# Twelve of 32 experts with 64 token slots and two weight products, the gated unit as one ScalarE function, and down weights in 8 KB pieces

## The reference

```python
logits = (hf @ w_router + b_router).astype(jnp.float32)
top_vals, top_idx = lax.top_k(logits, TOP_EXPERTS)     # 4 of 32
gates = jax.nn.softmax(top_vals, axis=-1)
...
gu = xb @ w_gu[e] + b_gu[e]                            # 1024 -> 2048
glu = jnp.minimum(gu[:, :D_EXPERT], SWIGLU_LIMIT)
lin = jnp.clip(gu[:, D_EXPERT:], -SWIGLU_LIMIT, SWIGLU_LIMIT)
act = glu * jax.nn.sigmoid(SWIGLU_ALPHA * glu) * (lin + 1.0)
return (act @ w_down[e] + b_down[e]) * g[:, None]      # 1024 -> 1024
```

## Time and profile before

| what | value |
|---|---|
| median of 3 runs | 1509.83 us |
| span of the profiled execution | 1508.6 us |
| the runs' times less that span | 0.8 to 3.4 us |
| TensorE busy | 1454.6 us, 96% |
| VectorE busy | 1310.3 us, 87% |
| ScalarE busy | 1105.7 us, 73% |
| GpSimd busy | 232.7 us, 15% |
| moved | 448.53 MB |
| granted TensorE clock | full in nearly all of the 40 slices |

### The profile page before, as it was taken

One profiled execution on the slowest core, in us unless ns is written; L12 is line 12 of the kernel. 1 busy time (PEld: TensorE's weight loads), 2 busy tenths in 40 slices (PEclk: granted clock), 3 DMA queues, 4 the chain that ended last, 5 costly groups with the idle time before them and its releaser, 6 DMA issues.

```text
span 1508.6 us, 18823 instructions
## 1 busy us (share of the span) xinstructions
PE 1454.6 (96%) x7148; PEld 1197.1 (79%) x7148; DVE 1310.3 (87%) x1320; ACT 1105.7 (73%) x1197; POOL 232.7 (15%) x120
## 2 busy tenths in 40 slices
PE   6999888999999999999999999999999999999996
PEld 5887767776788888888888888888888888888885
DVE  5799777558899999989999999999999999899995
ACT  5676654456778778887877788787787878887773
POOL 1122000011111121111111121111111211111101
PEclk9999979999999999999999999999999999999999
DMA  5422011178999999999999999999999999999991
GB/s 147 152 58 69 29 56 42 49 280 322 328 370 372 369 368 366 374 368 373 366 370 370 370 372 370 376 364 357 369 368 368 368 364 373 369 368 362 381 359 36
DMA packets 102307, 448.53 MB, mean 297 GB/s; under 512 B 18496, under 2 KB 23616, under 8 KB 69376
## 3 DMA queue, kind: packets, MB, share of 16 engines
q1 hardware_dynamic: 89808, 428.32, 73.4%
q0 software_dynamic: 9792, 18.90, 5.2%
q10 hardware_dynamic: 2608, 0.01, 0.1%
HBM read 440.89 MB, written 23.07 MB: 308 GB/s over the span
## 4 chain that ended last, share of the span: by engine, by line
PE 86%; DVE 9%; ACT 2%; issue 2%; DMA 1%; POOL 0%; POOLq 0%; ACTq 0%; DVEq 0%
PE ps L1948 68%; PE ps L1710 2%; PE ps L1712 2%; PE ps L1711 2%; PE ps L1958 2%; PE ps L1917 2%; PE ps L1722 2%; PE ps L1909 2%; DVE work L1388 1%; DVE nmax L1399 1%; PE ps L1813 1%; DVE top L1387 1%; DVE W L571 1%; DMA out_dram<-ysb 1%; PE ps L1784 0%
## 5 line engine op out<-in xcount | busy, mean ns | idle before, releaser
L776 DVE TENSOR_TENSOR whl<-wraw,whl 128x2048 fp32r<-128x2048 f32 x384 | 865.7, 2288 | 83.4 <-ACT whl L771 74.7
L771 ACT ACTIVATE whl<-wraw 128x2048 fp32r<-128x2048 f32 x384 | 732.8, 1919 | 206.5 <-PE ps L1948 206.5
L1948 PE MATMUL ps<-whl,xT 128*128 128x512 f32 x3120 | 730.6, 392 | 1.3 <-issue 1.3
L1948 PEld LDWEIGHTS ps<-whl,xT 128*128 128x128 f32 x3120 | 580.6, 188 | 122.8 <-issue 2.0
L1948 PE MATMUL ps<-whl,aT 128*128 128x512 f32 x1488 | 346.1, 391 | 0.6 <-DVE whl L776 0.6
L1948 PEld LDWEIGHTS ps<-whl,aT 128*128 128x128 f32 x1488 | 276.9, 188 | 57.0 <-DVE whl L776 1.0
L941 POOL DMA_INDIRECT out_dram<-ysb,idx x32 | 100.6, 3144 | 453.3 <-ACT ysb L1222 453.3
L932 POOL DMA_INDIRECT xg<-h_rows,idx x32 | 88.3, 2759 | 471.2 <-DVE idx L1606 463.6
L1710 PE MATMUL ps<-W,HT 128*128 128x512 f32 (+1 forms) x184 | 73.1, 397 | 5.8 <-DVE W L571 4.8
L1712 PE MATMUL ps<-W,HT 128*128 128x512 f32 (+1 forms) x184 | 70.1, 381 | 0.0
L1711 PE MATMUL ps<-W,HT 128*128 128x512 f32 (+1 forms) x184 | 69.8, 379 | 0.0
(11 more groups left out here) (246 smaller groups left out, 1377.0 us busy)
## 6 DMA issues: line engine op xcount, KB each, us to landing
wraw<-in_w_gu_dram SPq DMA_DIRECT2D x256, 1024.0 KB, 8.1
wraw<-in_w_down_dram SPq DMA_DIRECT2D x128, 1024.0 KB, 7.1
WR<-in_w_in_dram SPq DMA_DIRECT2D x20, 512.0 KB, 3.6
WR<-in_w_o_dram SPq DMA_DIRECT2D x8, 512.0 KB, 3.7
xs<-in_x_dram SPq DMA_DIRECT2D x4, 512.0 KB, 7.9
WR<-in_x_dram SPq DMA_DIRECT2D x4, 512.0 KB, 3.6
out_dram<-WR SPq DMA_DIRECT2D x4, 512.0 KB, 2.6
h_rows<-WR SPq DMA_DIRECT2D x4, 512.0 KB, 2.6
```

The source lines that it names most:

```text
L771: act.activation(whl[:, n % HL, 0, :], wraw[n % RAW], ACT.Copy).then_inc(chunk_hi, 1)
L776: eng.tensor_tensor(whl[:, n % HL, 1, :], wraw[n % RAW], whl[:, n % HL, 0, :].bitcast(F32), ALU.subtract).then_inc(chunk_lo, 1)
L1948: ins = pe.matmul(bank, a[x_][j], w[:, b, j, 512 * q:512 * q + 512], start=c == NG and j == 0 and n == 0, stop=last and j == nj - 1 and n ...
```

## The change

Twelve places in the order of experts (3, 5, 8, 10, 13, 15, 18, 20, 23, 25, 28, 30) become narrow: 64 slots. The experts are sorted by their token count when the program runs, and the twelve with fewest tokens go to the narrow places; experts 0 and 1 stay where they are (`FIXED`). SP reads the expert's number into a register for its loads.

A narrow expert's stationary operand holds the tokens' high parts in columns 0 to 63 and their low parts in columns 64 to 127. Products with the high and the low weights then give rows 0 to 63 and rows 64 to 127, eight matmuls in a chunk. Rows 64 to 127 are added to rows 0 to 63 by a fold: ScalarE copies the low rows out of PSUM (`gu_low_half`, `y_low_half`), and TensorE adds them with a shifted identity (`fold_gate_up`, four matmuls; `fold_down`, two).

The gated unit: x times sigmoid(1.702 x) becomes one ScalarE function; VectorE then takes its minimum with the value at the limit and multiplies by the linear half, one instruction instead of two. Down weights are read so that a partition gets 8 KB in one piece (rows 8p to 8p+7); to match, `turn_a` takes activations with a stride of eight.

```diff
-SIG_TOP = 1.0 / (1.0 + math.exp(-ALPHA * LIMIT))
-DENSE_AT = [(0, 3), (0, NG), (1, 1), (1, 5)]
+GLU_TOP = LIMIT / (1.0 + math.exp(-ALPHA * LIMIT))
+DENSE_AT = [(0, 5), (0, NG), (1, 2), (1, 5)]
 ROUNDS = SEQ // P
+
+
+FIXED = 2
+NARROW = sorted([5 * a + 3 for a in range(6)] + [5 * a + 5 for a in range(6)])
+WIDE = E - len(NARROW)
+HALFP = P // 2
+NOWHERE = 1.0e4
+
+
+def narrow(j):
+
+    return j in NARROW
 
 
 def build(nc, x, positions, g_attn, w_in, g_qa, g_ka, g_idx_k, lambda_q1, lambda_k1,
...
-        def chunk_src(e, c):
+        def chunk_src(e, c, at_=None):
+            if at_ is None:
+                at_ = e
             if c < NG:
-                return w_gu[0, e, c * P:(c + 1) * P, :]
-            return w_down[0, e].rearrange("(q j p) n -> q p j n", q=ND, j=2)[c - NG]
+                return w_gu[0, at_, c * P:(c + 1) * P, :]
+            return w_down[0, at_].rearrange("(p q j) n -> p q j n", q=ND, j=2)[:, c - NG]
 
         def slot_ps(j):
...
+            return len(NARROW) * r + NARROW.index(e)
+
+        def blocks_of(b):
+
+            return ps[:, TP + b, :].rearrange("p (k n) -> p k n", k=4)
+
+        def high_of(tile, j, b):
+
+            return tile[:, 0, 4 * b:4 * b + 4, 0:HALFP] if narrow(j) else tile[:, 0, 4 * b:4 * b + 4, :]
+
+        def low_of(tile, j, b):
+
+            return tile[:, 0, 4 * b:4 * b + 4, HALFP:P] if narrow(j) else tile[:, 1, 4 * b:4 * b + 4, :]
+
+        def turned_ps(j, b):
+
+            return blocks_of(b)[:, :, 0:HALFP] if narrow(j) else blocks_of(b)
+
         def dn_bank(e):
...
+                ids_at = {}
                 for e, c in chunks():
+                    if c == 0 and e >= FIXED:
+                        if is0(r) and e == FIXED:
+                            sp.wait_ge(ids_ok, 1)
+                        ids_at[e] = sp.value_load(ids[0:1, e:e + 1], min_val=0, max_val=E - 1)
                     if not is0(r) or chunk_no(e, c) >= RAW:
-                        load_chunk(sp, r, e, c)
+                        load_chunk(sp, r, e, c, ids_at.get(e))
 
...
+            def gu_low_half(r, e):
+
+                act.wait_ge(chunk_used, done(r, e, NG - 1))
+                act.wait_ge(act_ok, E * r + e)
+                act.activation(fold_gu[HALFP:P, :].rearrange("p (a n) -> p a n", a=4), ps[HALFP:P, GU:GU + 4, :],
+                               ACT.Copy).then_inc(gu_low, 1)
+
+            def y_low_half(r, e):
+
+                act.wait_ge(chunk_used, done(r, e, NCH - 1))
+                act.wait_ge(scattered, 16 * (T + E * r + e))
+                act.activation(fold_y[HALFP:P, :].rearrange("p (a n) -> p a n", a=2), ps[HALFP:P, DN:DN + 2, :],
+                               ACT.Copy).then_inc(y_low, 1)
 
             def turn_g_hi():
 
...
-            def sigmoid(r, e):
-                act.wait_ge(chunk_used, done(r, e, NG - 1))
-                after(act, act_ok, E * r + e)
-                act.activation(acts[:, 0, :].rearrange("p (a n) -> p a n", a=2), ps[:, GU:GU + 2, :], ACT.Sigmoid,
-                               scale=ALPHA).then_inc(sig_ok, 1)
+                    act.activation(high_of(a_of(e), e, b), turned_ps(e, b), ACT.Copy).then_inc(aT_hi, 1)
+
+            def gated(r, e):
+                if narrow(e):
+                    act.wait_ge(gu_folded, narrow_no(r, e) + 1)
+                else:
+                    act.wait_ge(chunk_used, done(r, e, NG - 1))
+                    after(act, act_ok, E * r + e)
+                act.activation(acts[:, 0, :].rearrange("p (a n) -> p a n", a=2), ps[:, GU:GU + 2, :],
+                               ACT.Gelu_apprx_sigmoid).then_inc(sig_ok, 1)
 
             def y_rows(r, e):
 
-                act.wait_ge(chunk_used, done(r, e, NCH - 1))
+                if narrow(e):
+                    act.wait_ge(y_folded, narrow_no(r, e) + 1)
+                else:
+                    act.wait_ge(chunk_used, done(r, e, NCH - 1))
                 act.wait_ge(gslot_ok, E * r + e + 1)
                 act.wait_ge(scattered, 16 * (T + E * r + e))
                 act.activation(ysb.rearrange("p (a n) -> p a n", a=2), ps[:, dn_bank(e):dn_bank(e) + 2, :], ACT.Copy,
...
+                        if c == 1 and i >= 2 and narrow(i - 2):
+                            y_low_half(r, i - 2)
                         if c == 3 and i >= 2:
                             y_rows(r, i - 2)
...
-                    sigmoid(r, i)
+                    if narrow(i):
+                        gu_low_half(r, i)
+                    else:
+                        gated(r, i)
                     if i + 1 < E:
                         turn_x_hi(r, i + 1)
                     split_hi(act, r, i - 1, NCH - 1)
+                    if narrow(i):
+                        gated(r, i)
                 split_hi(act, r, E - 1, NG)
...
+            def read_counts():
+
+                dve.tensor_copy(crow, ps[:, TP + 1, T * E:(T + 1) * E]).then_inc(counts_read, 1)
+
...
+            def place_experts():
+
+                dve.wait_ge(tables_ok, 2)
+                mine = pick[:, 0:E]
+                link(dve.scalar_tensor_tensor(out=key, in0=crow, scalar=2.0 * E, in1=tie, op0=ALU.mult, op1=ALU.add))
+                link(dve.tensor_tensor(held, key, mine, ALU.mult))
+                link(dve.tensor_reduce(kcol[:, 0:1], held, AX.X, ALU.add))
+                link(dve.tensor_scalar(key, key, kcol[:, 0:1], None, ALU.is_gt))
+                link(dve.tensor_reduce(kcol[:, 1:2], key, AX.X, ALU.add))
+                dve.tensor_scalar(spread[0:2 * E, 0:E], ordered[0:2 * E], kcol[0:2 * E, 1:2], None, ALU.is_equal)
+                link(dve.tensor_scalar(spread[2 * E:3 * E, E:2 * E], ordered[2 * E:3 * E], kcol[2 * E:3 * E, 1:2], None,
+                                       ALU.is_equal))
...
+            def placed():
+
+                at_ = ps[:, TP + 1, :]
+                dve.wait_ge(permuted_ps, 1)
+                dve.tensor_scalar(ids, at_[:, 2 * T * E:2 * T * E + E], 0.5, None, ALU.mult).then_inc(ids_ok, 1)
+                both = at_[:, 0:2 * T * E].rearrange("p (t a e) -> p t a e", t=T, a=2)
+                dve.tensor_scalar(rank[:, :, FIXED:E], both[:, :, 1, FIXED:E], -1.0, None, ALU.add) \
+                   .then_inc(rank_ok, 1)
+                link(dve.tensor_scalar(gden, both[:, :, 0, :], 0.5, None, ALU.mult))
+                for n in range(3):
...
-                dve.scalar_tensor_tensor(out=acts[:, 1, :], in0=acts[:, 0, :], scalar=SIG_TOP, in1=acts[:, 1, :],
-                                         op0=ALU.min, op1=ALU.mult).then_inc(prod_ok, 1)
-                dve.wait_ge(prod_ok, E * r + e + 1)
                 after(dve, aT_ps, 2 * E * r + 2 * e)
-                dve.scalar_tensor_tensor(out=acts[:, 2, :].rearrange("p (a n) -> p a n", a=2),
-                                         in0=ps[:, GU:GU + 2, :], scalar=LIMIT,
-                                         in1=acts[:, 1, :].rearrange("p (a n) -> p a n", a=2),
+                dve.scalar_tensor_tensor(out=acts[:, 2, :], in0=acts[:, 0, :], scalar=GLU_TOP, in1=acts[:, 1, :],
                                          op0=ALU.min, op1=ALU.mult).then_inc(act_ok, 1)
...
+                    read_counts()
+                    first_gates()
                     split_lo(dve, 0, 0, 0)
                 turn_x_lo(r, 0)
                 for c in range(1 if is0(r) else 0, NG):
                     split_lo(dve, r, 0, c)
-                    if c == 1:
+                    if is0(r) and c == 1:
+                        spread_gates()
+                    if c == 2:
                         slot_gates(r, 0)
                         slot_gates(r, 1)
+                    if is0(r) and c == 2:
+                        place_experts()
+                    if is0(r) and c == 3:
+                        turn_g_lo()
                     if is0(r) and c == 4:
-                        turn_g_lo()
+                        placed()
                 slot_rows(r, 2)
                 slot_gates(r, 2)
...
+                by_row = acts[:, 2, :].rearrange("s (p k) -> s k p", k=KD)
                 pe.wait_ge(act_ok, E * r + e + 1)
                 for b in range(2):
                     for k in range(4):
                         ins = pe.transpose(ps[:, TP + b, k * P:(k + 1) * P],
-                                           acts[:, 2, (4 * b + k) * P:(4 * b + k + 1) * P], ident)
+                                           by_row[:, 4 * b + k, :], ident)
                     ins.then_inc(aT_ps, 1)
 
...
+            def permute():
+
+                pe.wait_ge(spread_ok, 1)
+                pe.wait_ge(gT_lo, 1)
+                for t in range(T):
+                    for a in range(2):
+                        pe.matmul(ps[:, TP + 1, 2 * E * t:2 * E * t + 2 * E], gT[:, a, rows_of(t)], spread[0:3 * E, :],
+                                  start=(a == 0), stop=(a == 1))
+                first = 2 * T * E
```

(28 more changed lines are left out.)

207 lines of the change are left out of this document (151 added, 56 removed).

## The result

The changed kernel takes 1548.57 us (median of 4 runs, 1543.68 to 1554.12), the kernel before 1510.15 us on the same chip: ratio 1.025, 95% interval 1.023 to 1.0269. It is slower by 38 us; 1496 was forecast. The profiled execution took 1543.68 us, the shortest of the four; its span is 1541.9, those of the others go from 1546.7 to 1552.4. Where the text compares spans, it takes this one.

A forecast was written before the change was run, and what follows sets the result against it. TensorE was taken to bind, with VectorE and DMA 8% and 4% behind. Terms -130.8 + 30.0 + 44.4 + 24.0 + 9.6 + 2.4 + 6.9 = -13.5 on a 1508.6 span gave 1495.1, median 1496; range 1455 to 1522 us.

The forecast's parts named there:

- VectorE and ScalarE in an iteration: Expert phase: ScalarE's queue behind the fold delays chunks by iteration type, adding 44.4, 24.0 and 9.6 us.
- No wait, but ScalarE's 10.4: Iterations 3, 8, ... 28 (i narrow, i-2 wide): ScalarE's work makes chunk 7 late, 1.6 us each, 9.6 in all.
- TensorE's gain: Narrow experts: 576 fewer matmuls, -130.8 us; added folds of 1.55 and 0.95 us, +30.0, with 16.4 as lower bound.
- What ScalarE's queue adds: Delays before chunks in three iteration types: 7.4 us each in six, 4.8 in five, 1.6 in six.
- The start: First expert: ordering experts by count puts new small instructions among VectorE's splits, +6.9 us.
- The end: Last expert's down products: expert 30's removed matmuls (3.6 us) bring only VectorE's 1.2, so +2.4 us.
- Strided loads: TensorE's turn of activations with a stride of eight elements: taken as 0, with 23 us kept in the range.
- The rival that made 23 us of it: Turn of activations: each strided load costs 0.09 us more, 23 us in all, ending at 1519; chance 0.20.
- Nothing waits for DMA: Weight stream: 8 KB down pieces transfer quicker, 421 against 389 GB/s, but are worth 0 us.
- The rival of a stream held to 368 GB/s: Expert phase: DMA is the bound, iterations stay at 35.6 us and the start is added, 1517; chance 0.08.
- The gated unit: 0 directly: Activations after gate-up: one VectorE instruction of 1.21 us less, hidden behind 10.90 us of down work, 0 us.
- only the rates bind: First rival, expert phase: cheaper folds and half the stalls covered, 1443, say 1440 to 1475 us; chance 0.20.

The follow-up runs named there:

- c1: The kernel before, with only VectorE's reading of the token search moved ahead of its splits of the down chunks: 1510.23 us, ratio 1.0 to the kernel before.
- e1: The changed kernel, with VectorE reading the token search's results ahead of its down-chunk splits: 1500.2 us, ratio 0.9929 to the kernel before.
- e4: The changed kernel, with filler matmuls keeping TensorE at work ahead of chunk 4 and the turn of tokens: 1533.9 us, ratio 1.0154 to the kernel before.
- e2: The changed kernel, with ScalarE writing narrow experts' output rows later, behind the high parts of chunks 4 and 5: 1500.86 us, ratio 0.994 to the kernel before.
- e5: e3 plus four filler matmuls ahead of chunk 4 and four ahead of the turn of tokens: 1475.38 us, ratio 0.9776 to the kernel before.
- e7: e3 with down weights in 4 KB pieces and the contiguous turn of activations again: 1467.95 us, ratio 0.972 to the kernel before.
- e3: The changed kernel with both edits, e1's early search results and e2's late output rows: 1459.03 us, ratio 0.9668 to the kernel before.
- p1: The kernel before with only the new gated unit, 8 KB down pieces and the strided turn: 1507.06 us, ratio 0.9982 to the kernel before.

## Why the prediction was wrong

The step that failed is the list under "VectorE and ScalarE in an iteration": for i narrow, i-2 wide it says "No wait, but ScalarE's 10.4", and for i narrow behind a narrow i-2 it knows only the wait ahead of chunk 4. It followed the splits and the fold, and left out that TensorE's turn of tokens waits for what VectorE reads from the token search. In the wide kernel this came 1.0 us before it was needed, and making it earlier is worth nothing (c1). With chunks of 1.8 us TensorE arrives at the turn 5.8 us earlier, and VectorE, whose splits do not get faster, reads the result only 2.4 earlier. So the prediction put at nothing a wait of 2.5 us in eleven iterations and of about 1 in four, 31.8 us in all, with a slow chunk behind nine of them, another 14.

Taking the wait away (e1) gives 174.9 us for five iterations where the prediction's pieces give 174.6. By where it arose, the 46.8 us by which the forecast span was short are 45.9 between the biases of iterations 2 and 31, 1.5 at the end, and -0.6 at the start. e1 takes 47.5 off the first of these, so this one wait with what follows it is nearly the whole miss. The clock's part of it is 14 us by the repeats with and without a stretch, 12 by e4.

Step by step:
- TensorE's gain: right, chunks of eight take 1.8 us. The folds were priced too high: between its neighbours one of four adds 1.21 us and one of two 0.75, 23.5 us for all where 30.0 was summed. The lower bound was 16.4.
- What ScalarE's queue adds (7.4, 4.8 and 1.6 us): right in place and size; e1's iterations are within 0.3 us of the forecast ones, and e2 cuts TensorE's wait ahead of chunk 4 from 3.27 to 1.15.
- The start: 6.9 forecast, 6.3 measured at iteration 2, but with luck: from bias 0 on the change costs 8.8, and 2.5 came back from attention. The cost varies with the stretches at the lower clock between bias 0 and bias 2: with one of them (the kernel after, e2, e5, e7) this part takes 77.8 us, with two (e1, e4) 79.3, with three (e3) 80.6, and the kernel before, with none, takes 68.9. The prediction had no price for a stretch.
- The end: TensorE waits 3.0 us ahead of the last down products, where it waited 1.3 before, and starts them 1.3 us sooner after the last bias, where 1.2 was forecast. The part from the last bias on is still 60.7 us against 59.4, where a saving of 0.3 was forecast: the first of these chunks runs at the lower clock and takes 1.5 us longer.
- Strided loads: 0 taken, right for the time, but the load itself does get slower. The Trainium skill (SBUF — State Buffer, The DMA port swizzle) speaks of a penalty for accesses that each cross to a new line. The trace is in line with it for this load alone, 188 against 141 ns in p1, though contiguous loads of `xT` take 188 as well. The rival that made 23 us of it fell, since the time of the transposes does not hang on their loads.
- "Nothing waits for DMA": true of the changed kernel. At e3's pace it is nearly true, 2.9 us in six waits, and with 4 KB pieces no longer (e7). That 8 KB pieces move faster was read from 421 against 389 GB/s in two different stages; at the same work the share did not fall (p1). The rival of a stream held to 368 GB/s fell: e3 holds 389 over 990 us. The Trainium skill (DMA: Bandwidth & Descriptors, Specifications) gives about 358 GB/s per core; the trace is above it here.
- "The gated unit: 0 directly": 2 us in p1, but 24 us in e3, where VectorE has become one of the engines that TensorE waits for.
- The drop of the granted clock after waits stood nowhere in the prediction. It costs some 14 us between the biases of iterations 2 and 31 (12 by e4, with fillers that cost something themselves), 1.5 at the end, and some at the start.

Four recorded numbers are off, and nothing hangs on them: the first rival's sum is 1442.4 where it says 1443, ScalarE's 4 x 1.9 plus 3.0 is 10.6 and not 10.4, the margin of 1.1 us in c1's expectation is 1.0, and the 18 stretches between 390 and 1530 us in the expectations are 17.

The rival "only the rates bind" was close to what e3 reached (1459, forecast 1440 to 1475), but only after both moves in the queues. The change as made ended on the slower side for a reason that no rival named.

## What to carry to other kernels

When one engine's pieces get shorter, list every semaphore that it waits for in the shortened stretch, with its margin before, and not only those of the data that it multiplies. A margin of 1.0 us, invisible in a table of waits, became a wait of 2.5 us eleven times. Where an engine's queue holds a short instruction that another engine needs behind long work that it could do later, its place in the queue is worth more than its length: moving two such instructions took 48 of 1549 us off, and a move of the same kind on ScalarE another 41.
